# Unread products behind six norm sums of a fused two-block transformer kernel

## The chip, the cores and the metric

The kernel runs on one core of a Trainium2 chip. The metric is the device time of one execution in microseconds (us). Names of engines: TensorE multiplies, ScalarE does activations, VectorE elementwise work, GpSimd issues one stream of DMAs, SyncE issues the other.

## The reference, cut to what matters

Two blocks of two layers each run one after the other on a sequence of 512 tokens of width 1024 (the first block carries 256 context tokens as well, 768 in all). Each layer is a mixer (latent attention, gated linear attention, gated delta net, retention) and a feed-forward part, with norms between them:

```
# block 1, every layer: RMS norm of the input, then scale and shift
h = modulate(rms_norm(x, g), shift, scale);  x = x + gate * rms_norm(mixer(h), g1)
h = modulate(rms_norm(x, g2), shift2, scale2);  x = x + gate2 * rms_norm(sqrelu_mlp(h), g3)
# block 2, every layer: layer norm of the sum
x = layer_norm(ALPHA * x + (1 + g1) * mixer(x * (1 + sc1) + sh1))
x = layer_norm(ALPHA * x + (1 + g2) * conv_ffn(x * (1 + sc2) + sh2))
```

Everything is computed in float32 accuracy. Most large products are made as three products of rounded halves (`hi` times `hi`, `lo` times `hi`, `hi` times `lo`).

## The kernel before, in words

The activations lie feature by feature in SBUF: `xT` and `hT` hold 8 blocks of 128 features, with the tokens along the free axis. Each engine has one instruction stream written out by hand; semaphores order the streams.

**Weights.** SyncE loads them group by group into a ring of two buffers (`wring`). ScalarE rounds a group to `w_hi` (L1674), VectorE takes the rest, `w_lo` (L2335), each in two halves. TensorE waits for the half that it needs (`split_group`, `second_half`). In the first MLP of block 1, in the second one and in the first feed-forward part of block 2, VectorE also takes in pieces of the next layer's modulation weights (L2163, L2165), which GpSimd loads by DMA; in its stream they stand between the splits of the weights.

**Norms.** A norm over features is a sum over partitions. TensorE makes it: the stationary operand is the 128x128 block `ones` of the constant table `base_tab` (128x256: the identity beside the ones), the moving operand are the squares, and the sum lands in the PSUM bank `sc[:, 0, ...]`. `square_sum` (L768 for 768 tokens, L771 for 512) does this block by block for an input norm ("h0m", "h1", "h1m"). For the layer norms of block 2, `begin_sums` and `end_sums` (L796 to L805) make the sums of x and of its squares. The last product increments `n_used`. ScalarE then takes the deviation (Ln, Exp), VectorE multiplies, ScalarE scales, shifts and rounds each block to `x_hi`, VectorE makes `x_lo` of it (L2344, L2341), and TensorE, which has waited since the sum, begins the first group of the next stage: two outputs of 128 features with 8 blocks of input each, three products each (six for the 768 tokens, two halves of 384 columns). That group takes block k when `x_lo` of block k is there, and the group after it waits for its own `w_lo`.

**The bank.** `sc[:, 1, 0, :]` is the third of the four banks of `sc`. It is used inside attention, inside gated linear attention and in the gated delta net. Nobody reads what lies in it at the six places of the change. `mod_psum`, which collects modulation columns, is the bank beside it, `sc[:, 1, 1, :]`.

The six places, in order of time: "h0m" (in front of the first MLP, `mlp0`), "h1" (in front of gated linear attention, `gla_head`), "h1m" (in front of `mlp1`), and the layer norms "ln0" (in front of `ffn0_up`), "ln0f" (in front of `ret_head`) and "ln1" (in front of `ffn1_up`). The fourth layer norm, "ln1f", is the end of the kernel.

Of the kernel before, what the change touches and what calls it, by code (L numbers as in the profile page):

```python
# [12 lines left out]
P = 128  # L13
# [134 lines left out]
def first_and_second_block(nc, A, out):  # L148
    ctx = ExitStack()
    with ctx:  # L150
        def sb(name, shape, dt=F32):
            return ctx.enter_context(nc.sbuf_tensor(name, shape, dt))
# [14 lines left out]
        base_tab = sb("base_tab", [P, 2 * P])  # L167
        ident, ones = base_tab[:, 0:P], base_tab[:, P:2 * P]
# [42 lines left out]
        sc = ctx.enter_context(nc.psum_tensor("sc", [P, 2, 2, 512], F32))  # L211
# [205 lines left out]
        def unit(stage, j):  # L417

            return acc[:, (UNIT0[stage] + j) % 2]
# [63 lines left out]
        def emptied(eng, stage, it, j):  # L483

            u = UNIT0[stage] + j
            eng.wait_ge(acc_free[u % 2], u // 2 + 1 + it * (UNITS[stage] // 2))

        def claim(eng, stage, it, j):

            u = UNIT0[stage] + j  # L490
            if u >= 2:
                eng.wait_ge(acc_free[u % 2], u // 2 + it * (UNITS[stage] // 2))
# [8 lines left out]
        def ln_square(b):  # L501

            return sums[:, 2, :] if b % 2 == 0 else rstd[:, 0:SEQ]
# [223 lines left out]
        def _(pe):  # L727
            def group(stage, it, j, k, n):

                s = loaded(pe, stage, it, j)  # L730
                begun[0] = True
                return wring[s][:, 0:k * n].rearrange("p (k n) -> p k n", k=k)
# [15 lines left out]
            def linear(u, w, m, x, n, nk, rows=P, at=0, after=None):  # L748

                for k in range(nk):  # L750
                    block_ready(k, after)
                    if n == T:
                        for h in range(2):
                            last = mm(u[at:at + rows, h, 0:HALF], w[:, k, m:m + rows],
                                      x(k)[:, h * HALF:(h + 1) * HALF], k == 0, k == nk - 1)
                    else:
                        last = mm(u[at:at + rows, 0, 0:n], w[:, k, m:m + rows], x(k), k == 0, k == nk - 1)
                return last

            def square_sum(name, n, blocks=None):  # L760

                _, b0, nb = NORMS[name]
                for b in blocks or range(nb):
                    pe.wait_ge(n_sq, b0 + b + 1)
                    s = sq[:, (b0 + b) % 2]
                    if n == T:
                        for h in range(2):
                            last = pe.matmul(sc[:, 0, h, 0:HALF], ones, s[:, h * HALF:(h + 1) * HALF],  # L768
                                             start=b == 0, stop=b == nb - 1)
                    else:  # L770
                        last = pe.matmul(sc[:, 0, 0, 0:n], ones, s[:, 0:n], start=b == 0, stop=b == nb - 1)  # L771
                    last.then_inc(n_used, 1)
# [19 lines left out]
            def begin_sums(name, i):  # L792
# [4 lines left out]
                pe.wait_ge(n_used, NORMS[name][1] + DB - 1)  # L797
                pe.matmul(sc[:, 0, 0, :], ones, sq_total, start=True, stop=False)

            def end_sums(name, stage, i):  # L800

                emptied(pe, stage, *divmod(DB - 1, UNITS[stage]))
                pe.matmul(sc[:, 0, 1, :], ones, xT[:, DB - 1, CTX:T], start=False, stop=True).then_inc(n_mean, 1)
                pe.wait_ge(n_sq, NORMS[name][1] + DB)
                pe.matmul(sc[:, 0, 0, :], ones, ln_square(DB - 1), start=False, stop=True).then_inc(n_used, 1)  # L805

            seq_h = lambda k: hT[:, k, CTX:T]
            all_h = lambda k: hT[:, k, :]
# [87 lines left out]
            for h in range(2):  # L896
                last = pe.matmul(unit("mla_rope", 0)[:, h, 0:HALF], dup, kraw[0:64, h * HALF:(h + 1) * HALF],
                                 start=True, stop=True)
# [3 lines left out]
                      stop=True).then_inc(acc_ready, 1)  # L902
# [4 lines left out]
            pe.wait_ge(krope_ready, 2)  # L907
            S = "mla_pair"
            with pe.Fori(0, MLA_H // 2) as it:
                wq = group(S, it, 0, 3, 384)  # L910
                pe.wait_ge(uq_in, it * 48 + 48)
                for j, m in ((0, 0), (1, NOPE)):
                    claim(pe, S, it, j)
                    linear(unit(S, j), wq, m, lambda k: cq[:, k, :], T, 3).then_inc(acc_ready, 1)
                claim(pe, S, it, 2)
                linear(unit(S, 2), wq, 2 * NOPE, lambda k: cq[:, k, :], T, 3).then_inc(acc_ready, 1)
                wkv = group(S, it, 1, 2, 512)
# [14 lines left out]
                for j in range(2):  # L932
                    claim(pe, S, it, 8 + j)
                    pe.matmul(unit(S, 8 + j)[:, 0, 0:256], rot2, qraw[:, CTX + 256 * j:CTX + 256 * (j + 1)],
                              start=True, stop=True).then_inc(acc_ready, 1)
# [40 lines left out]
                for m in range(2):  # L976
                    last = pe.matmul(mod_psum[:, bass.ds(it * 2 + (COND_AT + m), 1)], cond_acc[:, m * P:(m + 1) * P], ones[:, 0:1],
                                     start=True, stop=True)
                last.then_inc(first_summed, 1)

            def split_group(stage, it, j, k, n):

                g = GROUP0[stage] + j
                pe.wait_ge(w_split, half_group(stage, it, j, 0))
                begun[0] = True
                return parts(g % 2, k, n)

            def second_half(stage, it, j):
                pe.wait_ge(w_split, half_group(stage, it, j, 1))

            def split_product(u, w, m, k, x, start, stop, rows=P):

                for h, n, hi, lo in x:
                    for i, (a, b) in enumerate(((0, hi), (0, lo), (1, hi))):
                        o = u[0:rows, h, 0:n] if len(b.shape) == 2 else in_two(u[:, h, 0:n])
                        last = mm(o, w[a][:, k, m:m + rows], b, start and i == 0, stop and i == 2)
                return last

            def turns(nk):

                together = [(v, k) for k in range(nk - 2) for v in range(2)]
                return together + [(v, k) for v in range(2) for k in range(nk - 2, nk)]

            def out_proj(stage, nk, per, squares=None, norm=None):
# [31 lines left out]
                if norm:  # L1036
                    end_sums(norm[0], stage, norm[1])
# [5 lines left out]
            def input_split(k, before):  # L1043

                pe.wait_ge(x_split, before + k + 1)

            def mlp(i, n):
                S = f"mlp{i}"
                if n == T:
                    spans = [(h, HALF, slice(h * HALF, (h + 1) * HALF)) for h in range(2)]  # L1050
                else:
                    spans = [(0, n, slice(0, n))]
                with pe.Fori(0, 4) as it:
                    w = split_group(S, it, 0, DB, 256)
                    for v in range(2):
                        claim(pe, S, it, v)
                    for v, k in turns(DB):
                        if v == 0:
                            input_split(k, 2 * DB * i)
                            if k == DB // 2:  # L1060
                                second_half(S, it, 0)
                        last = split_product(unit(S, v), w, v * P, k, x_parts(n, k), k == 0, k == DB - 1)
                        if k == DB - 1:
                            last.then_inc(acc_ready, 1)
                    for u in range(2, 16):
                        if u % 2 == 0:
                            w = split_group(S, it, u // 2, DB, 256)
                        claim(pe, S, it, u)
                        for k in range(DB):
                            if u % 2 == 0 and k == DB // 2:  # L1070
                                second_half(S, it, u // 2)
                            if u == 8:
                                pe.wait_ge(relu_free, it * DB + (4 * DB * i + k + 3))
                            x = x_parts(n, k) if u < 8 else [(h, w_, hid_hi[:, k, t], hid_lo[:, k, t]) for h, w_, t in spans]
                            last = split_product(unit(S, u), w, (u % 2) * P, k, x, k == 0, k == DB - 1)
                        last.then_inc(acc_ready, 1)
                        if u in MOD_SUM_AFTER:
                            mod_sum(i, it, MOD_SUM_AFTER[u], 2 - i)

            square_sum("h0m", T)  # L1080
            pe.wait_ge(mod_ready, 2)
            mlp(0, T)
            added_sum("y0m", T, True)


            square_sum("h1", T)
            S = "gla_head"
            order = ([0, 1, 2, 3, 4], [1, 0, 5, 4, 3])

# [129 lines left out]
            head_sum(GLA_H)  # L1219
            out_proj("gla_out", DB, 2, ("y1", SEQ))  # L1220
            square_sum("h1m", SEQ)
            mlp(1, SEQ)
            added_sum("y1m", SEQ)

# [20 lines left out]
            for r in range(2):  # L1245
                for c in range(LT):
# [5 lines left out]
                      stop=True).then_inc(d_cols, 1)  # L1252
# [193 lines left out]
            with pe.Fori(0, RET_H) as it:  # L1446
# [16 lines left out]
                for g in range(2):  # L1463
                    w = split_group(S, it, 2 + g, DB, 256)
                    for t in range(LT):
                        j, i = divmod(t, 2)
# [1527 lines left out]
```

## Time and profile before

| what | value |
|---|---|
| median of 3 runs | 3748.09 us (3744.73 to 3749.03) |
| the profiled execution, its own time | 3753.23 us |
| its span, first to last instruction | 3751.5 us |
| mean granted TensorE clock | 0.973 of full speed |

The profile is a trace of one execution. Its rows give the busy time of an engine, the start and length of single instructions, what released an engine that had waited, and the clock that was granted to TensorE, as a share of 2.4 GHz (1.00 is 2.4 GHz, 0.50 is 1.2 GHz). A float32 product shows as two records, one for each of its two instructions. A product of rounded halves is one record. The length of a record contains the time until its result has landed, so that records overlap; the time that one costs is the distance between starts. In rows of groups the numbers behind the bar are the busy time in us, the mean length of one record in ns, and the idle time before. In rows of a stretch (`from:to`) stand its length, the busy time of TensorE's products, of its weight loads, of VectorE, of ScalarE and of GpSimd (each with the number of instructions), then the granted TensorE clock (PEclk), the share of the DMA engines and GB/s. Rows of the timeline give start, length and instruction, and in brackets the idle time before it and what ended it.

### The profile page before, as it was taken

How to read it: one execution, taken by the hardware profiler on the slowest of the kernel's cores; microseconds unless marked ns; L12 is line 12 of the kernel's file. 1: busy time of each engine (PE TensorE's matmuls, PEld its weight loads, DVE VectorE, ACT ScalarE, POOL GpSimd, SP SyncE). 2: the span in 40 equal slices, each digit the busy share in tenths (PEclk: the TensorE clock that was granted, in tenths of full speed). 3: DMA queues.
4: the chain of work that ended last, by engine and by line, in shares of the span. 5: the costliest groups of instructions: out<-in, count | busy, mean ns of one | idle time of the engine just before them, and what ended most of it. 6: DMA issues, size and time to landing. Idle time of an engine off the chain costs nothing.

```text
span 3751.5 us, 45103 instructions
## 1 busy us (share of the span) xinstructions
PE 3512.0 (94%) x17014; PEld 2820.2 (75%) x17014; DVE 1917.2 (51%) x2755; ACT 1194.3 (32%) x1545; POOL 211.6 (6%) x374
## 2 busy tenths in 40 slices
PE   7999889999997998899999999789998999899998
PEld 3566679999995887677846665678877777678876
DVE  4555546445446564644445665577745333454434
ACT  3033424213224342533322333243323222333332
POOL 0111001001000000111100000011100000000000
PEclk9999999999998999999999999899999999999999
DMA  6212114234221111444421111045533222122222
GB/s 209 80 58 65 49 36 133 93 99 127 91 85 41 40 56 56 135 157 154 157 68 35 34 34 45 23 140 181 181 108 101 67 73 73 56 84 96 89 84 84
DMA packets 294723, 335.30 MB, mean 89 GB/s; under 512 B 16465, under 2 KB 264145, under 8 KB 294481
## 3 DMA queue, kind: packets, MB, share of 16 engines
q1 hardware_dynamic: 261552, 232.93, 19.7%
q0 software_dynamic: 29440, 96.49, 8.1%
q10 hardware_dynamic: 3617, 4.26, 0.4%
q8 instruction: 83, 1.36, 0.2%
q14 instruction: 31, 0.25, 0.0%
HBM read 331.55 MB, written 2.10 MB: 89 GB/s over the span
## 4 chain that ended last, share of the span: by engine, by line
PE 86%; DVE 6%; ACT 2%; DMA 2%; issue 2%; ACTq 0%; DVEq 0%; POOL 0%; SPq 0%; POOLq 0%
PE acc L737 64%; PE sc L737 6%; PE sc L1318 2%; DMA wring<-in_mlp_w 1%; PE acc L962 1%; PE sc L878 1%; PE sc L942 1%; PE acc L1318 1%; PE acc L1498 1%; PE sc L944 1%; DVE w_lo L2335 1%; DVE arena L2093 1%; DVE xT L2097 0%; DVE d_col L2284 0%; PE acc L953 0%
## 5 line engine op out<-in xcount | busy, mean ns | idle before, releaser
L737 PE MATMUL acc<-x_lo,w_hi 128*128 128x512 f32 (+1 forms) x2144 | 810.1, 378 | 31.3 <-DVE d_out_lo L2312 9.2
L2335 DVE TENSOR_TENSOR w_lo<-wring,w_hi 128x1024 fp32r<-128x1024 f32 (+2 forms) x400 | 441.7, 1146 | 560.1 <-ACT w_hi L1674 560.1
L1674 ACT ACTIVATE w_hi<-wring 128x1024 fp32r<-128x1024 f32 (+2 forms) x400 | 377.4, 991 | 996.6 <-DMA wring<-in_mlp_w 483.1
L737 PEld LDWEIGHTS acc<-x_lo,w_hi 128*128 128x128 f32 x2144 | 408.5, 191 | 95.4 <-DVE w_lo L2335 25.4
L737 PE MATMUL acc<-hid_hi,w_hi 128*128 128x512 f32 (+1 forms) x1120 | 415.0, 371 | 18.6 <-DVE w_lo L2335 9.3
L737 PE MATMUL acc<-hid_hi,w_lo 128*128 128x512 f32 (+1 forms) x1120 | 410.7, 367 | 0.0
L737 PE MATMUL acc<-x_hi_holes,w_hi 128*128 128x512 f32 x704 | 282.1, 401 | 15.3 <-DVE x_lo L2341 13.9
L737 PE MATMUL acc<-x_hi_holes,w_lo 128*128 128x512 f32 x704 | 278.5, 396 | 0.0
L737 PE MATMUL acc<-hid_lo,w_hi 128*128 128x384 f32 (+1 forms) x768 | 272.2, 354 | 0.0
L737 PEld LDWEIGHTS acc<-hid_hi,w_hi 128*128 128x128 f32 x1120 | 212.0, 189 | 48.0 <-DVE arena L2371 11.8
L737 PE MATMUL acc<-x_hi_seq,w_hi 128*128 128x512 f32 x576 | 228.1, 396 | 16.2 <-DVE x_lo L2344 13.7
L737 PEld LDWEIGHTS acc<-hid_hi,w_lo 128*128 128x128 f32 x1120 | 211.8, 189 | 24.8
L737 PE MATMUL acc<-x_hi_seq,w_lo 128*128 128x512 f32 x576 | 225.2, 391 | 0.0
L737 PE MATMUL acc<-x_hi,w_hi 128*128 128x384 f32 (+1 forms) x608 | 208.6, 343 | 11.2 <-DVE x_lo L2344 6.2
L737 PE MATMUL acc<-x_hi,w_lo 128*128 128x384 f32 (+1 forms) x608 | 207.4, 341 | 0.0
L737 PE MATMUL acc<-wide_lo,w_hi 128*128 128x512 f32 x480 | 188.6, 393 | 0.0
L737 PE MATMUL sc<-hT,wring 128*128 128x512 f32 x384 | 177.7, 606 | 0.5 <-DVE d_col L2561 0.5
L723 POOL DMA_DIRECT2D rows_or_mod<-in_ada_w x176 | 94.9, 539 | 1421.3 <-DVE xT L2778 605.0
L737 PEld LDWEIGHTS acc<-x_hi_holes,w_hi 128*128 128x128 f32 x704 | 133.5, 190 | 48.1 <-issue 16.1
L2165 DVE SCALAR_TENSOR_TENSOR tab<-rows_or_mod,cs,tab 128x512 f32<-128x512 f32 x204 | 147.9, 748 | 30.8 <-DMA rows_or_mod<-in_ada_w 27.4
L737 PEld LDWEIGHTS acc<-x_hi_holes,w_lo 128*128 128x128 f32 x704 | 133.6, 190 | 32.5
L737 PEld LDWEIGHTS acc<-hid_lo,w_hi 128*128 128x128 f32 x768 | 145.0, 189 | 9.8
(416 smaller groups left out, 5930.7 us busy)
## 6 DMA issues: line engine op xcount, KB each, us to landing
wring<-in_mlp_w SPq DMA_DIRECT2D x64, 1024.0 KB, 5.4
rows_or_mod<-in_ada_w POOLq DMA_DIRECT2D x208, 256.0 KB, 3.1
wring<-in_ffn_up SPq DMA_DIRECT2D x44, 1024.0 KB, 5.1
wring<-in_ret_w_in SPq DMA_DIRECT2D x24, 1024.0 KB, 5.2
rstd<-in_ada_w POOLq DMA_DIRECT2D x88, 256.0 KB, 3.4
wring<-in_ffn_down SPq DMA_DIRECT2D x32, 704.0 KB, 4.7
wring<-in_gdn_w_in SPq DMA_DIRECT2D x16, 1024.0 KB, 5.8
tab<-in_ada_w POOLq DMA_DIRECT2D x40, 256.0 KB, 3.4
```

The source lines that it names most:

```text
L723: pool.dma_start(mod_w[s], w[:, k, bass.ds(it * (per * MOD_N) + i * MOD_N, MOD_N)]).then_inc(mod_loaded[s], 16)
L737: ins = pe.matmul(o, lhsT, rhs, start=start, stop=stop)
L878: last = pe.matmul(mod_psum[:, bass.ds(it * (MOD_PIECES[phase] // DB * per * nv) + c, 1)], mod_acc[:, i % 2, v, m * P:(m + 1) * P], ones[: ...
L942: pe.matmul(sc[:, n % 2, h, 0:w], qn[:, e, t * P:(t + 1) * P], kn[:, e, k0:k0 + w], start=True, stop=False)
L944: last = pe.matmul(sc[:, n % 2, h, 0:w], qr[:, t * P:(t + 1) * P], krope[:, e, k0:k0 + w], start=False, stop=True)
L962: last = pe.matmul(unit(S, 11 + 2 * n)[:, 0, 0:P], vtok[:, k, e * P:(e + 1) * P], probT[:, n % 2, k * P:(k + 1) * P], start=k == 0, stop=k ...
L1318: last = pe.matmul(o[:, e, t], left[:, e, t], right[:, e, t], start=True, stop=True)
L1498: last = pe.matmul(unit(S, 8 + j)[:, i, t * P:SEQ], r_v[:, t, m // CTX, m % CTX:m % CTX + P], r_s[:, t, 0:SEQ - t * P], start=t == 0, stop ...
L1674: f(w_hi[s][:, c], wring[s][:, c], ACT.Copy).then_inc(w_high, 1)
L2093: st.did(tt(y[:, b + 1], y[:, b + 1], rstd[:, 0:n], MUL))
L2165: ins = stt(a, mod_w[s], cs[:, k, v:v + 1], a, MUL, ADD)
L2335: tt(w_lo[s][:, c], wring[s][:, c], w_hi[s][:, c].bitcast(F32), SUB).then_inc(w_split, 1)
```

## The change

A helper `spare` issues products of `ones` with the whole table `base_tab` (256 columns, float32) into columns 0 to 255 of `sc[:, 1, 0, :]`. Sixteen of them stand behind the last sum of the layer norms ln0, ln0f and ln1, nine behind the sums of the input norms h0m, h1 and h1m. They wait for nothing and increment nothing. Nothing else is changed.

```
+            def spare(count):
+
+                for _ in range(count):
+                    pe.matmul(sc[:, 1, 0, 0:2 * P], ones, base_tab[:, :], start=True, stop=True)
+
             def end_sums(name, stage, i):
...
                 pe.matmul(sc[:, 0, 0, :], ones, ln_square(DB - 1), start=False, stop=True).then_inc(n_used, 1)
+                if i < 3:
+                    spare(16)
...
             square_sum("h0m", T)
+            spare(9)
             pe.wait_ge(mod_ready, 2)
             mlp(0, T)
...
             square_sum("h1", T)
+            spare(9)
...
             square_sum("h1m", SEQ)
+            spare(9)
             mlp(1, SEQ)
```

## Rows read from the trace of the kernel before

**Rows 1.** The page: busy us (share of the span), instructions

```profile
PE 3512.0 (94%) x17014; PEld 2820.2 (75%) x17014; DVE 1917.2 (51%) x2755; ACT 1194.3 (32%) x1545; POOL 211.6 (6%) x374
```

**Rows 2.** Whom TensorE waited for: us in total, times, longest us

```profile
PE acc L737 <- DVE x_lo L2344: 19.9, 3, 9.2
PE acc L737 <- DVE x_lo L2341: 13.9, 2, 7.0
```

**Rows 3.** Stretches: gap, then slow start, of h0m, h1, h1m, ln0, ln0f, ln1

```profile
556.70:562.90 6.20, 0.03 (x1) 0.06 (x1) 3.83 (x5) 5.05 (x7) 0.00 (x0) 0.83 0.00 0
562.90:567.50 4.60, 4.60 (x15) 4.60 (x16) 4.10 (x5) 4.50 (x8) 0.00 (x0) 0.50 0.54 154
1151.80:1158.00 6.20, 0.02 (x1) 0.00 (x1) 3.77 (x5) 5.00 (x7) 0.00 (x0) 0.73 0.00 0
1158.00:1161.40 3.40, 3.37 (x10) 2.49 (x11) 2.90 (x4) 3.34 (x6) 0.00 (x0) 0.50 0.02 5
1518.80:1523.30 4.50, 0.04 (x1) 0.00 (x0) 2.97 (x6) 3.56 (x6) 0.00 (x0) 1.00 0.00 0
1523.30:1526.70 3.40, 3.36 (x8) 2.73 (x9) 3.18 (x6) 3.34 (x6) 0.00 (x0) 0.50 0.31 75
2466.40:2473.30 6.90, 0.00 (x0) 0.00 (x0) 6.78 (x12) 4.29 (x7) 0.00 (x0) 0.67 0.00 1
2473.30:2478.90 5.60, 5.55 (x13) 4.42 (x14) 5.60 (x10) 5.15 (x8) 0.00 (x0) 0.50 0.60 187
2866.00:2875.30 9.30, 0.07 (x2) 0.06 (x1) 9.13 (x14) 6.08 (x9) 0.00 (x0) 0.62 0.48 169
2875.30:2878.30 3.00, 3.00 (x7) 2.43 (x8) 3.00 (x6) 2.61 (x5) 0.00 (x0) 0.50 0.28 83
3341.80:3348.70 6.90, 0.00 (x0) 0.00 (x0) 6.79 (x12) 4.36 (x7) 0.00 (x0) 0.81 0.00 0
3348.70:3352.90 4.20, 4.16 (x10) 3.32 (x11) 4.20 (x8) 3.78 (x6) 0.00 (x0) 0.51 0.47 145
```

**Rows 4.** Float32 products of 256 columns; two stretches of h1's `square_sum` (L768)

```profile
L737 PE MATMUL acc<-wring,arena 128*128 128x256 f32 x96 | 21.4, 379 | 0.0
...
1140.00:1141.00 1.00, 1.00 (x3) 0.57 (x2) 1.00 (x2) 0.57 (x1) 0.00 (x0) 0.50 0.00 0
1141.00:1142.00 1.00, 1.00 (x4) 0.60 (x4) 1.00 (x3) 0.27 (x1) 0.00 (x0) 1.00 0.00 0
```

**Rows 5.** Timeline: last `x_lo`, and first product behind the first group (h0m, h1m)

```profile
576.31 0.96 DVE L2344 TENSOR_TENSOR x_lo<-hT,x_hi 128x768 fp32r<-128x768 f32 x1 [1.12 <-ACT x_hi L1563]
...
581.75 0.33 PE L737 MATMUL acc<-x_hi,w_hi 128*128 128x384 f32 x1
...
1532.08 0.69 DVE L2344 TENSOR_TENSOR x_lo<-hT,x_hi_seq 128x512 fp32r<-128x512 f32 x1 [0.68 <-ACT x_hi_seq L1563]
...
1535.92 0.39 PE L737 MATMUL acc<-x_hi_seq,w_hi 128*128 128x512 f32 x1
```

**Rows 6.** Timeline, ln1: the next `w_lo`, first product behind the first group

```profile
3359.63 2.36 DVE L2335 TENSOR_TENSOR w_lo<-wring,w_hi 128x1024 fp32r<-128x1024 f32 x2 [1.67 <-ACT w_hi L1674]
...
3361.87 0.40 PE L737 MATMUL acc<-x_hi_holes,w_hi 128*128 128x512 f32 x1
```

**Rows 7.** Timeline, ln0: the next `w_lo`, first product behind the first group

```profile
2487.41 2.36 DVE L2335 TENSOR_TENSOR w_lo<-wring,w_hi 128x1024 fp32r<-128x1024 f32 x2
...
2488.69 0.50 PE L737 MATMUL acc<-x_hi_holes,w_hi 128*128 128x512 f32 x1 [1.40 <-DVE w_lo L2335]
```

**Rows 8.** Stretches around two shorter gaps inside the second MLP

```profile
1580.60:1582.70 2.10, 0.00 (x0) 0.00 (x0) 2.10 (x4) 0.05 (x1) 0.00 (x0) 1.00 0.00 0
1582.70:1587.00 4.30, 4.25 (x19) 3.52 (x20) 2.67 (x4) 0.00 (x0) 1.62 (x3) 1.00 0.55 176
1605.80:1607.40 1.60, 0.00 (x0) 0.00 (x0) 1.60 (x3) 0.00 (x0) 0.00 (x0) 1.00 0.00 0
1607.50:1612.00 4.50, 4.50 (x13) 3.52 (x14) 0.54 (x1) 0.00 (x0) 0.00 (x0) 0.63 0.55 170
```

More of the change, by code:

```diff
@@ L798, in begin_sums, with spare @@
                 pe.matmul(sc[:, 0, 0, :], ones, sq_total, start=True, stop=False)
+            def spare(count):
+                for _ in range(count):
+                    pe.matmul(sc[:, 1, 0, 0:2 * P], ones, base_tab[:, :], start=True, stop=True)
             def end_sums(name, stage, i):
@@ L805, in end_sums @@
                 pe.matmul(sc[:, 0, 0, :], ones, ln_square(DB - 1), start=False, stop=True).then_inc(n_used, 1)
+                if i < 3:
+                    spare(16)
             seq_h = lambda k: hT[:, k, CTX:T]
@@ L1080, in _ @@
             square_sum("h0m", T)
+            spare(9)
             pe.wait_ge(mod_ready, 2)
@@ L1086, in _ @@
             square_sum("h1", T)
+            spare(9)
             S = "gla_head"
@@ L1221, in _ @@
             square_sum("h1m", SEQ)
+            spare(9)
             mlp(1, SEQ)
```

## The prediction

> **What bounds the kernel now.** I read the page first, then the list of TensorE's waits, then stretches around each place of the change, then single instructions there. TensorE is busy for 94% of the span [rows 1], so a microsecond taken from its path is worth having only where its own work is the path. Its waits for `x_lo` are among its longest: five of the six places stand in the two rows, 33.8 us together [rows 2] (the sixth, h1, is filed under the gate's product; its gap is in the stretches). The change fills these gaps and does not shorten them: they end when VectorE delivers `x_lo`. What it can alter is the clock behind them. In each of the six places TensorE is idle for 4.5 to 9.3 us, the granted clock falls from 1.00 to 0.50 in the gap or at its end, and the products behind the gap start at the lower level, 1.2 GHz [rows 3]. The slow starts last 4.6, 3.4, 3.4, 5.6, 3.0 and 4.2 us, 24.2 us in all [rows 3].
>
> **What a slow start costs at most.** At the lower level a product of 512 columns costs 5.55 us / 13 = 0.43 us [rows 3]. At the upper one it costs about 0.23: in ln1 some 38.5 products lie between 3352.9 and 3361.87, 8.97 us [rows 3, 6]. So a slow start of length L holds work of 0.54 L, and a full recovery gives back 0.46 x 24.2 = 11.1 us. That is the upper end of what can be won, and three things cut it.
>
> **Price of the added products.** A float32 product of 256 columns shows as two records, and 96 records kept TensorE busy for 21.4 us: 0.223 us a record, 0.446 us a product [rows 4]. Sixteen are 7.14 us, nine are 4.01 us; all six places together 3 x 7.14 + 3 x 4.01 = 33.5 us of work inside 40 us of gaps. The sum has landed at the start of each gap in rows 3, and the pipe is free about 0.1 us earlier, so the fill ends: h0m and h1 6.2 - 3.9 = 2.3 us before the next product; h1m 4.5 - 3.9 = 0.6 us before; ln0 and ln1 7.0 us into 6.9 us, 0.1 us late; ln0f 9.3 - 7.0 = 2.3 us before. The lateness of 0.1 us costs nothing: there TensorE takes the blocks faster than VectorE supplies them, and catches up. I take 0 for the added products, with 0.2 us as the upper bound. Behind them in TensorE's queue stands only the first group, which waits for VectorE anyway. Nobody waits for the bank, and `n_used` is incremented before the fill.
>
> **First cut: supply.** With a warm clock the group can't end before its last `x_lo` and the products behind it.
> - h0m: the last `x_lo` lands at 577.27, the product on it can start 0.14 later as the first one does, and 18 products of 384 columns follow it (one block of the first output, two of the second). One costs 0.173 us by the steady part of the group, (581.75 - 567.5) / 82. The group ends at 577.41 + 3.12 = 580.5 in place of 581.75: 1.25 us won, where a full recovery would be 2.1 [rows 3, 5].
> - h1m: 1532.77 + 0.15 + 9 x 0.228 = 1535.0 against 1535.92: 0.95 us, of 1.6 [rows 5].
> - ln1: a full recovery of 1.9 us would let the next group start at 3360.0. But that group needs the first half of its `w_lo`, and the pair of halves runs from 3359.63 for 2.36 us, so the first lands at about 3360.85: the group starts at 3360.9 in place of 3361.87, 1.0 us [rows 6].
> - ln0f is fed by VectorE in the same manner; of its 0.46 x 3.0 = 1.4 us I take half, about the share that h0m, h1m and ln1 keep: 0.65 us [rows 3].
> - h1 has 15 products a block (gate, query and key), 12 x 0.173 + 3 x 0.228 = 2.8 us, where h0m with 12 keeps VectorE's pace, so it recovers all: 0.46 x 3.4 = 1.6 us [rows 3].
>
> **Second cut: ln0 gives nothing.** Its group would end more than 1 us earlier too. But the group behind it already waits 1.40 us, until 2488.69, for a `w_lo` that VectorE starts at 2487.41 [rows 7]. In VectorE's stream modulation pieces stand in front of it, each of which waits for a DMA that GpSimd issues once the norm is done. None of that is moved by TensorE's clock. The wait grows by what the clock saves: 0. If TensorE's start there came later, 1.4 us would be covered.
>
> **Third cut: does the filled gap hold the clock?** Where the fill leaves 0.6 us or nothing (h1m, ln0, ln1), TensorE is as busy as in any stretch at 1.00, and I take the clock as held. Where it leaves 2.3 us (h0m, h1, ln0f), the trace shows both outcomes for gaps as short: behind a gap of 2.2 us the clock stayed at 1.00, and behind one of 1.8 us it fell, a mean of 0.63 over the next 4.5 us [rows 8]. I count half for these three.
>
> The Trainium skill (TensorE: Matmul & The Clock Gate, "Why this matters for your kernels") asks only that idle gaps between bursts of matmuls be kept to a few microseconds at most. By that rule all six places hold. The trace differs here, since a gap of 1.8 us was followed by the lower level [rows 8]; by the rule the sum below would be 5.45 us in place of 3.7.
>
> **Sum.** Sure: h1m 0.95 + ln1 1.0 = 1.95 us. Half of (1.25 + 1.6 + 0.65 = 3.5) = 1.75 us. ln0 0, added work 0. Together 3.7 us less. The profiled execution took 3753.23 us with a span of 3751.5; with the change it would be 3749.5. It ran 5.1 us above the median of the three timed runs, 3748.09, and the sum is a difference, so I take it off the median: 3744.4 us. A measurement of this kernel can tell 0.2% from no change, 7.5 us, so this is no change that can be measured.
>
> What is won must survive later waits. Most of them (for squares, for outputs taken from PSUM, for the weights' splits) follow TensorE's own progress and move with it. In `mlp1` VectorE's order mixes weight splits with pieces that wait for DMAs, so the 0.95 us of h1m may be lost, or the waits there shift by a microsecond or two either way. I leave it in the sum and put it into the range.
>
> **The rivals.**
> 1. *All filled gaps hold the clock* (1.25 + 1.6 + 0.95 + 0 + 0.65 + 1.0 = 5.45 us): 3742.6. For it speaks the 2.2 us gap that held, against it the 1.8 us gap that did not [rows 8]. It is the skill's rule as worked out above.
> 2. *Full recovery:* supply and `w_lo` follow sooner than I read, 11.1 us: 3737. Against it: VectorE's rhythm is its own and doesn't depend on TensorE.
> 3. *Nothing arrives:* the short gaps lose the clock, and `mlp1`'s DMA waits and the next splits eat the rest: 3748.
> 4. *Slower: the products don't hold the clock.* It decides if the lower level comes while they still run. From the means of rows 3 the clock lasts 0.34 x 6.9 = 2.3 us into ln0's gap, 0.24 x 9.3 = 2.2 us into ln0f's and 0.62 x 6.9 = 4.3 us into ln1's. The fill behind these points costs double: ln0 (7.1 - 2.3) = 4.8 us more, so 4.9 us late, of which 1.4 are covered; ln0f 4.9 more, less 2.3 spare, 2.6 late; ln1 2.8 more, 2.9 late; the fills of nine end in time. 3.5 + 2.6 + 2.9 = 9.0 us: 3757. Against it: in h1's `square_sum` TensorE ran nothing but products of the same stationary ones with float32 squares, and under them the clock rose from 0.50 to 1.00 [rows 4], so such products count. What is new is the moving operand, half of it an identity, the other half ones.
>
> In a sentence by itself: the Trainium skill (TensorE: Matmul & The Clock Gate, "Part 4: PE-mode transpose") says that transposes against an identity don't count as busy in the same way; if that held for plain products with an identity as operand, rival 4 would be the outcome, and no row above shows it.
>
> **How the numbers follow.** The forecast (between 2 and 5 us less, one or two of the short gaps held) 0.45; rival 1 0.17; rival 2 0.10; rival 3 0.20; rival 4 0.08. The forecast and rivals 1 and 3 lie within 7.5 us of the median before, 0.82, though runs before spread over 4.3 us by themselves, which moves some 0.06 of it over either bound. Rival 2 is faster by over 0.2%, rival 4 slower. So faster 0.14, same 0.76, slower 0.10. The range takes in rivals 1 and 3 and the most of rival 2, and on the slow side the spread of the runs: 3738 to 3752.
>
> **What would show it.** Right: 150 new records of 256 columns, 223 ns apart; the clock at 1.00 through the gaps of ln0 and ln1 and the first group behind them at 0.23 us a product; small waits for `x_lo` between its first blocks; at ln0 the wait for `w_lo` grown from 1.40 us to about 2.5; ends of the first groups earlier by 1.25 (if held), 0.95 and 1.0 us. Wrong: records 430 ns apart, or a first product behind a fill later than its `x_lo` by over 0.2 us. The forecast falls if the ends of the groups move by less than 0.5 us, or if waits inside `mlp1` and the feed-forward parts grow by as much as the starts gained.

## The result, and the profile after

The median after is 3758.46 us (12 runs, 3750.02 to 3764.19) against 3748.44 before (12 runs, 3741.69 to 3752.7). The ratio is 1.0026, with a 95% interval of 1.0017 to 1.0035: the kernel became 10 us slower where I forecast 3.7 us faster. The profiled execution took 3758.84 us, 5.6 us more than that of before; the missing 4.4 us belong to the first profile of before, which ran 4.8 us above the median of that kernel; the last experiment comes back to it.

The page of the changed kernel, lines of its head, of the busy times, of the clock by slices and of the DMA queues. They answer to [rows 1]:

```profile
span 3757.2 us, 45403 instructions
PE 3546.3 (94%) x17164; PEld 2847.8 (76%) x17164; DVE 1918.0 (51%) x2755; ACT 1193.6 (32%) x1545; POOL 211.4 (6%) x374
PEclk9999999999998999999999999899999999999999
q8 instruction: 85, 1.39, 0.2%
```

Nothing here shows the loss. TensorE's share is the same, and its busy time grew by 34 us, the added products. The last line is a queue that the profile calls `instruction`: 85 packets of 16 KB; in the profile of before it has 83.

**Where it went.** I matched TensorE's products of the two traces one by one, leaving out the added ones, and took the difference of their starts (us after the start of the span; plus is later than in before).

| at, in before | what stands there | changed kernel | difference since the line above |
|---|---|---|---|
| 540 | inside the norm h0m | -0.48 | |
| 590 | second group of `mlp0` | -1.07 | -0.6 |
| 705 | first product behind the first jump back of `mlp0`'s loop | +1.11 | +2.2 |
| 1120 | end of `mlp0`, three jumps passed | +12.50 | +11.4 |
| 1158, 1165 | before and behind h1's gap | +11.88, +11.85 | -0.6 |
| 1523, 1537 | before and behind h1m's group | +10.62, +10.75 | -1.1 |
| 1806 | end of the third pass of `mlp1` | +1.31 | -9.4 |
| 2464, 2496 | before and behind ln0 | +6.13, +7.77 | +6.5 |
| 2875, 2890 | before and behind ln0f | +6.55, +5.92 | -1.9 |
| 3340, 3370 | before and behind ln1 | +6.15, +5.30 | -0.6 |
| 3740 | the end | +5.32 | 0 |

The loss stands in `mlp0`. Of the +4.8 us between 1806 and 2464 (+1.31 to +6.13), 4.4 build up in the gated delta net, in low-clock stretches that come and go between profiles: in three of those below, one of them of the unchanged kernel, the same part adds 0.2 us or less. `mlp0` is a loop of four passes, so TensorE jumps back three times. The timeline of before, around the first jump and at the second: start, length, instruction, and in brackets the idle time ahead of it and what ended it.

```profile
703.52 0.34 PE L737 MATMUL acc<-hid_hi,w_lo 128*128 128x384 f32 x1
704.95 0.41 PE L737 MATMUL acc<-x_hi,w_hi 128*128 128x384 f32 x1 [1.09 <-DVE arena L2368]
844.86 0.41 PE L737 MATMUL acc<-x_hi,w_hi 128*128 128x384 f32 x1 [1.09 <-DVE arena L2368]
```

The same of the changed kernel, all three jumps:

```profile
702.45 0.34 PE L737 MATMUL acc<-hid_hi,w_lo 128*128 128x384 f32 x1
702.82 0.95 DVE L2378 TENSOR_TENSOR arena<-arena,acc 128x768 f32<-128x768 f32 x1 [8.30 <-PE acc L737]
706.05 0.44 PE L737 MATMUL acc<-x_hi,w_hi 128*128 128x384 f32 x1 [3.27 <-issue]
850.30 0.65 PE L737 MATMUL acc<-x_hi,w_hi 128*128 128x384 f32 x1 [3.82 <-issue]
994.49 0.69 PE L737 MATMUL acc<-x_hi,w_hi 128*128 128x384 f32 x1 [3.76 <-issue]
```

In both kernels the first product of a pass needs the bank that VectorE empties behind the last product of the pass before. That takes 1.09 us and is all that the kernel before waits. In the changed one VectorE is done at 702.82 + 0.95 = 703.77, and the product comes 2.3 us later. "issue" means that it waited for nothing that the profile shows. The stretches behind the first jump show the second part of the price, the clock (columns: stretch, its length, TensorE's busy time and products, granted clock, DMA share, GB/s):

```profile
705.00:706.00 1.00, 0.00 (x0) 1.00 0.00 0
706.00:707.00 1.00, 0.94 (x5) 1.00 0.44 102
707.00:708.00 1.00, 1.00 (x5) 0.50 0.58 203
709.00:710.00 1.00, 1.00 (x5) 0.50 0.94 289
710.00:711.00 1.00, 1.00 (x6) 0.79 1.06 363
711.00:712.00 1.00, 1.00 (x8) 1.00 0.57 199
```

Behind the longer gap the clock is at the lower level for 3.4 us, which costs 1.6 us by the matched starts; behind the third jump it is there for 6.8 us, which costs 2.8. Three jumps cost 2.2 + 2.7 + 2.7 us of waiting and 1.6 + 1.6 + 2.8 us at the lower level: 13.6 us. They turn a lead of 1.07 us at 590 into a lag of 12.5 us.

**What the sequencer did.** The instructions of the loop line itself (`with pe.Fori(0, 4)`: L1053 before, L1060 after), for the three jumps; the numbers are shortest, median and longest duration in ns. Before, then after:

```profile
L1053 PEldq COMPARE_BRANCH  x3: 3273/3337/3478, 700.7 to 980.5; - x3
L1053 PEldq FUSED_REGOPS  x3: 50/50/50, 704.1 to 983.8; - x3
```

```profile
L1060 PEldq COMPARE_BRANCH  x3: 3297/3553/3613, 699.6 to 987.6; - x3
L1060 PEldq FUSED_REGOPS  x3: 50/50/50, 703.0 to 991.2; - x3
```

The jump itself takes 3.3 to 3.6 us in both, because the loop's first block of instructions has to be fetched again (where no packet moves, in a run below, it takes 0.21 us). TensorE's instruction stream runs some 3 us ahead of its products (the jump at 699.6, the last product of the pass at 702.45), so before, this was hidden but for the 1.09 us that VectorE needs anyway. In the changed kernel there is more. The instruction queue's DMA records have one packet at 700.55, right behind the jump (699.6), and the next at 703.63. Between them run only the three instructions at the head of the loop, at 702.97 and 703.08 (register arithmetic) and at 703.18 (the wait for the bank). The product behind them starts at 706.05, 2.4 us behind the second packet's start, as the head starts 2.4 us behind the first's. In before, the second packet starts at 704.69 and the products at 704.95: they don't wait for it.

So the three head instructions lie at the end of one block and the first product at the start of the next, and every jump waits for two fetches in a row. What moved them there are the 36 instructions of h0m's nine products (each two multiplies and two weight loads), which stand directly ahead of the loop.

### The profile page after: what moved, and what is told of

It reads as the page before. It is cut to its first block, busy times and chain, and to the rows that moved or that the text cites. A ratio compares the mean times of both kernels' runs of the same rounds, so it can differ in the third digit from the quotient of the medians.

```text
span 3757.2 us, 45403 instructions
## 1 busy us (share of the span) xinstructions
PE 3546.3 (94%) x17164; PEld 2847.8 (76%) x17164; DVE 1918.0 (51%) x2755; ACT 1193.6 (32%) x1545; POOL 211.4 (6%) x374
## 4 chain that ended last, share of the span: by engine, by line
PE 86%; DVE 6%; ACT 3%; DMA 2%; issue 2%; ACTq 0%; DVEq 0%; POOL 0%; POOLq 0%; SPq 0%
PE acc L737 64%; PE sc L737 6%; PE sc L1328 2%; DMA wring<-in_mlp_w 1%; PE acc L969 1%; PE sc L885 1%; PE sc L949 1%; PE acc L1328 1%; PE acc L1508 1%; PE sc L951 1%; DVE w_lo L2345 1%; DVE xT L2773 1%; DVE d_col L2294 0%; DVE arena L2103 0%; PE acc L960 0%
## 5 line engine op out<-in xcount | busy, mean ns | idle before, releaser
L737 PE MATMUL acc<-hid_hi,w_hi 128*128 128x512 f32 (+1 forms) x1120 | 413.4, 369 | 12.5 <-DVE w_lo L2345 9.3
```

What stands on the lines that cost most here:

```text
L737: ins = pe.matmul(o, lhsT, rhs, start=start, stop=stop)
```

## The experiments

Theory A is what stands above. B: the products themselves cost the time. C: chance, or the transfers of `mlp1`. "Jump wait" is the idle time ahead of the first product of a pass. All edits are shown against the changed kernel, unless said otherwise.

### Without h0m's fill, and with it alone

```
             square_sum("h0m", T)
-            spare(9)
```

> All the fills of the change but the nine products behind the sums for h0m, so that mlp0's loop begins at the instruction where it began in the kernel before. Theory A (36 more instructions ahead of the loop move it, and each of its three jumps back then stalls on instructions): the three waits at the jumps back are again 1.1 us instead of 3.3 to 3.8, the first sum behind mlp0 comes at 1126 us of the span and not at 1138, and the time is at or a little below the kernel before (ratio to before 0.998 to 1.001). Theory B (the products themselves, their work or the clock that they leave, cost the time): only a small part goes with nine products of 75, the waits at the jumps stay above 3 us, and the ratio stays at 1.002 to 1.003. Theory C (the loss is chance, or lies in transfers of mlp1 and later): mlp0 is as in the changed kernel or changes without order.

Measured: 3747.19 us, ratio 0.9998 (0.9989 to 1.0007). Jump waits 1.09, 1.09, 1.09 us, ended by VectorE. `mlp0` ends 0.5 us earlier than in before. Taking 9 of 75 products away takes the whole loss away.

```
             square_sum("h0m", T)
             spare(9)
...
             square_sum("h1", T)
-            spare(9)
...
             square_sum("h1m", SEQ)
-            spare(9)
...
-                if i < 3:
-                    spare(16)
```

> Only the nine products behind the sums for h0m, nothing else of the change. Theory A: the three jumps back of mlp0 wait 3.3 to 3.8 us each, the end of mlp0 comes 12 us later than before, and of it some 10 us reach the end where mlp1 doesn't take them back: ratio 1.0015 to 1.004. Theory B: nine products cost at most 4 us of work if nothing hides them, ratio below 1.001. Theory C: no change, ratio 1.000.

Measured: 3758.42 us, ratio 1.003 (1.002 to 1.0041). Jump waits 3.30, 3.79 and 3.76 us. These nine alone make the whole loss. C falls with the two runs, and so does B unless these nine are special.

### The same instructions without the work, and with a block of instructions

Both edits of this part are to the kernel with h0m's fill alone.

```
+            def narrow(count):
+
+                for _ in range(count):
+                    pe.matmul(sc[:, 1, 0, 0:1], ones, base_tab[:, 0:1], start=True, stop=True)
...
             square_sum("h0m", T)
-            spare(9)
+            narrow(9)
```

> As the kernel with only the h0m fill, but each of the nine products has one column and not 256: the same 36 instructions at the same place, with next to no work (4 us of TensorE's busy time become under 1). Theory A: the jumps back of mlp0 wait 3.3 to 3.8 us as with the wide products, and the ratio to before is the same 1.0015 to 1.004. Theory B: the cost goes with the work, the jumps wait 1.1 us, ratio 1.000.

Measured: 3760.13 us, ratio 1.0038 (1.0023 to 1.0052). Jump waits 3.30, 3.79, 4.04 us. B falls: the number of instructions counts, not their work. (The narrow products were not as cheap as I wrote: 18 records in 2.06 us. What a narrow record costs stands at the end.)

```
             square_sum("h0m", T)
             spare(9)
+            narrow(55)
```

> As the kernel with only the h0m fill, and behind it 55 more products of one column, so that 64 products, 256 instructions, stand ahead of mlp0's loop. Theory A in its narrow form (what counts is where the loop begins within blocks of 256 instructions, the size that the Trainium skill gives, page Runtime: NRT & Kernel Launch, section Instruction fetch mechanics): the waits at the jumps are again 1.1 us; the 220 narrow instructions themselves take 5 to 12 us once ahead of the loop, so the first group starts later by that, and the end of mlp0 is later by no more than that. Theory A in its wide form (any code ahead of the loop stalls it): waits of 3.3 us or more, and the end of mlp0 later by 12 us and the narrow products. Theory B: waits of 1.1 us, and the cost of 64 products once.

Measured: 3761.83 us, ratio 1.0044 (1.0027 to 1.006). Jump waits 1.09, 1.09, 1.09 us. `mlp0` itself is as long as in before, within 0.1 us; the start of it is 15.7 us later than in before, from the padding alone (110 narrow records, which took longer than the 5 to 12 us that I gave them), and 15.5 us of that reach `mlp1`. 36 instructions cost three waits, 256 cost none. That is the narrow form of A: what counts is the loop's place within blocks of 256 instructions (16 KB).

### How the place decides

The next four runs followed from a count. A pass of the loop shows 1694 recorded instructions. If three lie ahead of the cut with nine products, then 39 do in before: the loop starts at place 217 of its block (256 - 39). With n products ahead it starts at 217 + 4n, modulo 256. From place 217, 1694 instructions touch eight blocks; from a place up to 98 they touch seven.

```
             square_sum("h0m", T)
-            spare(9)
+            spare(14)
```

> The whole change, but 14 products behind the sums for h0m and not nine: 56 instructions ahead of mlp0's loop. In the run with 55 narrow products more, a shift by 256 instructions brought the wait at the jump back to 1.09 us, so what counts is where in a block of fetched instructions the loop's first instruction lies. Theory A1 (in the changed kernel the loop's three first instructions lie at the end of one block and its first product at the start of the next, so that each jump fetches two blocks one after the other): with 20 instructions more, head and products lie in one block, and the waits at the jumps are 1.1 us or less. Theory A2 (the loop is also fetched anew only because its 1694 instructions touch eight blocks; beginning near a block's start it touches seven and stays): the jumps wait nothing, 0.2 us from product to product, and mlp0 lasts 3 to 4 us less than before. Theory A3 (every move of the loop costs, except one by a whole block): 3 us or more. The 14 products fill the gap at h0m, so the clock stays at 2.4 GHz there. Ratio to before by A1 0.998 to 0.9995, by A2 0.997 to 0.9985, by A3 1.002 to 1.003.

Measured: 3741.16 us, ratio 0.9985 (0.9976 to 0.9994). Place 17. Jump waits 1.09, 1.09, 1.09 us, and not one block is fetched in the three passes. Of A2 the first half holds (the loop stays) and the second falls (the waits don't go): the 1.09 us are VectorE's bank, so `mlp0` is as long as before. The clock held at h0m. A3 falls.

The next three have only narrow products at h0m and no other fill: `narrow(5)`, `narrow(30)` and `narrow(40)`.

> Only five products of one column behind the sums for h0m, 20 instructions. Theories A1 and A2: the block's end lies 16 instructions, eight products (1.4 us), behind the loop's head, so a jump waits 1.1 us, then eight products run, then TensorE waits again 0.5 to 1.5 us for the next block; mlp0 is 2 to 5 us longer than before. Theory A3: one wait of 3 us or more at the jump.

Measured, one run: 3755.18 us. Three products of the timeline behind the first jump:

```profile
703.01 0.41 PE L737 MATMUL acc<-x_hi,w_hi 128*128 128x384 f32 x1 [1.10 <-DVE arena L2379]
704.30 0.34 PE L737 MATMUL acc<-x_lo,w_hi 128*128 128x384 f32 x1
706.01 0.45 PE L737 MATMUL acc<-x_hi,w_lo 128*128 128x384 f32 x1 [1.37 <-issue]
```

From 703.01 to 704.30 eight products start, then TensorE waits 1.37 us. Place 237 leaves 19 instructions: three of the head and 16, which are eight products. The count is right to the product. The later jumps wait 1.00 and 0.72 us there, and `mlp0` is 4.0 us longer than in before, inside the 2 to 5 us expected.

> Only 30 products of one column behind the sums for h0m, 120 instructions: the loop begins some 81 instructions into a block. A2: the loop touches seven blocks (81 + 1695 is under 1792), no block is fetched at its jumps, and they wait nothing. A1: they wait 1.1 us. A3: 3 us or more. The 30 narrow products take 5.6 us at 0.185 us a record, hidden behind the wait of 6.2 us for x_lo.

Measured, one run: 3751.57 us. Place 81: no block fetched, jump waits 1.09, 1.09 and 1.10 us. A2's statement on the fetches holds, that on the waits doesn't. The 30 products were not hidden as I had expected: they took 9.0 us instead of 5.6 and start the first group 2.9 us later.

> Only 40 products of one column behind the sums for h0m, 160 instructions: the loop begins some 121 instructions into a block. A2: 121 + 1695 is over 1792, the loop touches eight blocks and is fetched anew at each jump, wait 1.1 us as in the kernel before. A1: 1.1 us. A3: 3 us or more.

Measured, one run: 3760.09 us; the padding starts the loop 7.1 us later than in before. Place 121: nine blocks are fetched in each pass, jump waits 1.10, 1.09, 1.09 us. Between 30 and 40 products the loop no longer stays, as the count says.

### One product more

```
             square_sum("h0m", T)
-            spare(9)
+            spare(10)
```

> The whole change with one product more: ten behind the sums for h0m, not nine. By the runs so far mlp0's loop is not fetched anew where it begins early in a block, and its head and first product are cut apart where nine products stand ahead of it. Four instructions more put the loop's first instruction one behind a block's end (if the head of the loop holds three instructions before the cut, as the trace of the changed kernel shows them). Theory A: no block is fetched at the jumps back, the waits there are 1.1 us as in the kernel before, mlp0 is no longer than before, ratio to before 0.998 to 1.000, so one product more takes 10 us away. If it is not exactly so, one instruction of the loop can still lie before the cut, and the jumps fetch as before, with waits of 1.1 us or up to 3.8 us. Theory B (the cost belongs to the products and goes with their number): 1.003.

Measured: 3744.67 us, ratio 0.9999 (0.999 to 1.0008). Place 1. The jump of this kernel, in the order of the fences above: its branch, then the first product of the second pass.

```profile
L1060 PEldq COMPARE_BRANCH  x3: 207/208/209, 697.8 to 977.6; - x3
```

```profile
702.03 0.41 PE L737 MATMUL acc<-x_hi,w_hi 128*128 128x384 f32 x1 [1.09 <-issue]
```

The branch takes 0.21 us in place of 3.55. DMA packets and the instruction queue's share of them, for the second pass of the loop, in the changed kernel (699.6 to 843.3):

```profile
DMA packets 10249, 14.83 MB, mean 103 GB/s; under 512 B 512, under 2 KB 8704, under 8 KB 10240
q8 instruction: 9, 0.15, 0.5%
```

and in the kernel with ten (697.8 to 837.7), where the queue has no line, since it moved nothing:

```profile
DMA packets 10240, 14.68 MB, mean 105 GB/s; under 512 B 512, under 2 KB 8704, under 8 KB 10240
```

Nine products cost 10 us; ten cost nothing that can be measured. The clock fell at h0m with ten as with nine (the gap left is 1.90 us), so it is not the clock that takes the 10 us away.

### What the fills are worth without the loop's price

`spare(14)` at h0m and no other fill:

> Only the 14 products behind the sums for h0m, no other fill. What the fill is worth where the loop doesn't pay: the clock held at h0m takes 1.2 us from the first group, the loop itself is as long as before, so ratio 0.9990 to 1.0005. If the run with 14 and all the other fills (0.9985) had its gain from the loop that stays, this one has it too: 0.998 to 0.999.

Measured: 3748.03 us, ratio 1.0009 (1.0 to 1.0018). h0m's group ends 1.2 us earlier than in before (starts at 540 and 590 differ by -2.05 and -3.22 us), and nothing of it shows in the time; the ratio lies above the range that I gave. That speaks against the staying loop as the source of the 0.9985 above.

```
             square_sum("h0m", T)
-            spare(9)
+            spare(14)
...
             square_sum("h1", T)
-            spare(9)
+            spare(14)
...
             square_sum("h1m", SEQ)
-            spare(9)
+            spare(10)
...
                 if i < 3:
-                    spare(16)
+                    spare((16, 21, 16)[i])
```

> The version that the runs point to: 14 products at h0m (the loop stays) and at h1, ten at h1m, 16, 21 and 16 in the layer norms, so that the products reach to x_lo in every gap. Against the run with 14 at h0m and nine at h1 it also holds the clock at h1 (the gap of 2.33 us that was left there let it fall for 3.4 us, 1.0 to 1.7 us of time). Expected ratio 0.997 to 0.999; if the gain of the run before was chance, 0.999 to 1.000; if the fills give back nothing at the ends of the groups, no better than 0.9985.

Measured: 3744.72 us, ratio 1.0002 (0.9991 to 1.0012). The version meant to be the best is no better than before. It is the run with 14 at h0m and longer fills at three other places, so I don't take that run's 0.9985 for a gain: its interval reaches 0.9994, this one's begins at 0.9991, and one of the ten ratios in this document may lie that far out.

The kernel before, once more, unchanged:

> The kernel before itself, run as if it were another: what the measurement tells from no change, and a second profile. Expected ratio 1.000 within 0.001. Its profiled execution shows whether mlp1's waits and low-clock stretches (7 to 10 us more in the first profile of before than in every run since, whatever it changed) belong to the kernel or to that one execution: if to the execution, the second has mlp1 shorter by 5 us or more; if to the kernel, the two profiles agree there within 2 us.

Measured: 3747.9 us, ratio to itself 1.0006 (0.9997 to 1.0015). Between the products at 1545 and 1806 us of before, its second profile runs 4.7 us shorter than the first. It lies a little under the 5 us that I had set for "belongs to the execution", and far from the 2 us of the other case. So half of the 9.4 us that the changed kernel seems to regain in `mlp1` is the first profile of before being slow there. The spans agree: 5.6 us between the two profiled executions and 4.7 of this make 10.3, and the medians differ by 10.0.

## Why the prediction was wrong

**The step that failed** is "I take 0 for the added products, with 0.2 us as the upper bound. Behind them in TensorE's queue stands only the first group". It counted their time in the gap, and that was right: they end 2.33, 2.33 and 0.61 us ahead of the next product at h0m, h1 and h1m, where I had 2.3, 2.3 and 0.6. It did not count that 36 instructions stand ahead of a loop. None of the rivals had it: rival 4 gave almost the right time (3757) by a mechanism that did not occur. The 150 records are there, and the clock stayed at 1.00 under all of them. The lost term is +13.6 us in `mlp0`, shown by removal, by addition, by the same instructions without their work, and by one product more.

The rest of the sum, as the products ahead of and behind each group show it:

| place | forecast | changed kernel | filled to the end (14, 14, 10, 16, 21, 16) |
|---|---|---|---|
| h0m | -1.25 if held | -0.6, clock fell | -1.2, held |
| h1 | -1.6 if held | 0, clock fell | -1.55, held |
| h1m | -0.95 | +0.1, held | -0.8 |
| ln0 | 0 | +1.6 | +2.5 |
| ln0f | -0.65 | -0.6, held | -0.6 |
| ln1 | -1.0 | -0.85, held | -0.85 |

**The supply cuts were right** at h0m and h1 for the longer fill, and at ln0f and ln1. At h1m the changed kernel was 1.5 us ahead inside the group (at 1530: +9.10, at 1523: +10.62). The supply took 0.6 us of it (+9.72 at the group's last product, 0.9 us ahead, as forecast), and the start of the next group the rest, since there it waits for `w_lo`, which the sum did not have:

```profile
1546.56 0.49 PE L737 MATMUL acc<-x_hi_seq,w_hi 128*128 128x512 f32 x1 [0.75 <-DVE w_lo L2345]
```

The run with ten products at h0m kept only 0.1 us of it; in the three other runs that have this fill 0.8 to 0.9 us stayed.

**One of the three short gaps held:** of those with 2.33 us left, ln0f's kept the clock, h0m's and h1's lost it. That ln0f's held was luck: with the same fill and the same 2.33 us it held in the changed kernel and with ten products at h0m, and lost it without h0m's fill and with 14, where the group gained nothing. h1's lost it in all four of these runs. Only where the fill left 0.6 us or less did the clock hold in every profile. Three stretches of one microsecond behind h0m's fill, in the changed kernel and then with 14 products:

```profile
561.00:562.00 1.00, 0.00 (x0) 1.00 0.00 0
563.00:564.00 1.00, 1.00 (x6) 0.82 0.08 16
565.00:566.00 1.00, 1.00 (x5) 0.50 0.98 256
```

```profile
561.00:562.00 1.00, 1.00 (x6) 1.00 0.00 0
563.00:564.00 1.00, 0.82 (x5) 1.00 0.00 0
565.00:566.00 1.00, 1.00 (x7) 1.00 0.47 121
```

A product of 384 columns costs 0.32 us in the one and 0.17 us in the other. I had counted half of each of the three, 1.75 us, and got 0.6 + 0 + 0.6. So the rule of the Trainium skill that I had weighed against the trace (page TensorE: Matmul & The Clock Gate, section "Why this matters for your kernels"), gaps of a few microseconds at most, does not describe h0m and h1 here: 2.33 us was enough to lose the clock, and 1.90 us in the run with ten. It did no harm to the sum.

**ln0 was right in its mechanism and wrong in its price.** The wait for `w_lo` grew from the 1.40 us of [rows 7], but to 3.27 and not to 2.5, and the longer wait let the clock fall behind it (the changed kernel; the last three lines are stretches):

```profile
2494.87 0.50 PE L737 MATMUL acc<-x_hi_holes,w_hi 128*128 128x512 f32 x1 [3.27 <-DVE w_lo L2345]
```

```profile
2494.00:2496.00 2.00, 1.13 (x4) 0.90 0.62 199
2496.00:2498.00 2.00, 2.00 (x6) 0.50 0.66 200
2498.00:2500.00 2.00, 2.00 (x8) 0.75 0.95 301
```

The group was 1.8 us ahead at 2480 (+4.31 against +6.13), level at the wait (+6.18), and 1.6 us behind at 2496 (+7.77). The slow start was not removed but moved behind the wait. The same shows in every run that has this fill (+1.3 to +2.5 us); in the runs without it the same stretch is as long as in before, within 0.2 us.

Together the fills gain 0.6 + 0.6 + 0.85 and lose 1.7 us in the changed kernel, next to nothing, and the loop's 10 to 13 us stand alone. That agrees with 0.9998 for the kernel without h0m's fill.

**What a page says, and what the runs say of it.** The Trainium skill (Runtime: NRT & Kernel Launch, "Instruction fetch mechanics") states that instructions come in blocks of 16 KiB, 256 instructions, into a memory that for TensorE holds 2048; that crossing a block is mostly hidden; and that a taken branch whose target is not in the "current 2-page window" waits for a fetch. I had not weighed it: it is the rule that speaks against this change. The blocks of 256 and the fetch behind a jump agree with the runs here, and so does the 2048: seven blocks and one fetched ahead are eight. The window of two pages does not: `mlp0`'s jump leads from the seventh block of the loop back to the first with no fetch when the loop starts at place 1, 17 or 81 of a block, and the gated delta net's loop, 1188 recorded instructions long, fetches nothing in any run. For this case the rule would be that a loop stays if it touches at most seven blocks, and that rests on seven places of one loop.

**Not tried:** a place from 82 to 120, which would narrow the limit, or another loop of this length; and whether `mlp0`'s 1.09 us go if VectorE empties the bank sooner. Between 1545 and 1806 us `mlp1` lasts from 7.3 us less to 3.2 us more than in the second profile of before. TensorE's waits there sum to 2.5 to 10.9 us, and the clock is at the lower level for 6.8 us in three profiles and never in the others. What decides that stays open.

## What to carry to other kernels

Count instructions added ahead of a long loop like work: look at how long the loop's branch takes, and at whether the instruction queue moves packets in every pass. If it does, the loop is near the limit of what stays, and where it starts in a block of 256 decides between nothing, a hidden fetch of some 3.3 us and an open one of 2.2 to 2.7 us more at each jump, with 1.6 to 2.8 us at the lower clock behind it; a few instructions ahead of it move it from one to another. And a gap that is filled to hold the clock gives back only what the next wait leaves: at ln0 the slow start came back behind the wait, dearer.

## What I had not expected of the hardware

**Busy is not the same as clocked up.** Thirty narrow products (one column each, the same stationary operand) behind h0m's sums kept TensorE busy without a gap, and the granted clock still fell:

```profile
558.00:559.00 1.00, 1.00 (x11) 1.00 0.00 0
559.00:560.00 1.00, 1.00 (x7) 0.54 0.00 0
561.00:562.00 1.00, 1.00 (x6) 0.50 0.00 0
```

They had begun at 554.89. Under the 14 wide products, as busy by the same column, it stayed at 1.00. The identity in half of the wide products' moving operand did no harm: the clock was at 1.00 in every stretch under them. A narrow record costs 0.09 us at the upper level (11 a microsecond) and 0.155 at the lower, against 0.223 for one with 256 columns, so a column less is hardly a saving here. Their weight load alone has a record of 0.19 us.

**The price of a jump has two values and is hidden.** Over all runs the same branch takes 0.21 us or 3.3 to 3.8 us, and the profile's waits don't name it: they say "issue", or name the engine that happened to be later.
